# A hybrid RWKV and attention step on one core: output tiles made three at a time in the order of the input rows, and the next pair's r and v loaded in thirds

## The reference

```python
# layer 0, rwkv7_time_mix
r, k, v = rkv[0], rkv[1], rkv[2]
def step(S, inp):
    r_t, w_t, k_t, v_t, na_t, b_t = inp
    sa = jnp.einsum('bhvk,bhk->bhv', S, na_t)
    S = S * w_t[:, :, None, :] + sa[..., None] * b_t[:, :, None, :] + v_t[..., None] * k_t[:, :, None, :]
    return S, jnp.einsum('bhvk,bhk->bhv', S, r_t)
s_final, out = lax.scan(step, s0.astype(f32), xs)
...
out = (out + bonus.reshape(B, T, D)) * g
y = (out @ w_out.astype(f32)).astype(xn.dtype)
...
# layer 1, chunk_attention_prompt and chunk_attention_sample
return out @ w_out, ...
...
# every layer
hp = hp + yp
hp = hp + swiglu_ffn(rms_norm(hp, norm_ffn[layer]), ffn_w_gu[layer], ffn_w_down[layer])
```

## Time and profile before

| | us |
|---|---|
| timed runs, median of 3 | 3863.48 |
| timed runs, lowest and highest | 3858.71, 3866.56 |
| the profiled execution | 3859.63 |
| its span | 3857.9 |
| recurrence, first load to last gated store | 442.6 to 1198.8 |
| RWKV output projection, first load to first load of the next phase | 1202.9 to 1346.4 |
| attention's output projection, wide part | 2886.9 to 2953.7 |

### The profile page before, as it was taken

The page is one execution under the profiler, slowest core; times in us unless marked ns, Lnnn a source line. Parts: engine busy times, 40 slices in busy tenths (PEclk is TensorE's granted clock), DMA queues, the critical chain, the costliest instruction groups (busy, mean ns, idle before and its releaser), DMA issues. The chain is left out here.

```text
span 3857.9 us, 82894 instructions
## 1 busy us (share of the span) xinstructions
PE 3558.3 (92%) x34886; PEld 3286.7 (85%) x34886; DVE 1286.3 (33%) x2473; ACT 1002.5 (26%) x2041; POOL 1663.8 (43%) x1186
## 2 busy tenths in 40 slices
PE   7999778888885999999999999999979999999998
PEld 6999567777764999999999877777749999999997
DVE  5112456667752321122122422222232321221223
ACT  5212334445431110000000334444451100000003
POOL 5434355545532544435444543333326354444434
PEclk9999789999995999999999999999989999999999
DMA  3422101111103111111111223323331111111111
GB/s 141 136 90 83 61 22 36 46 42 36 36 23 131 40 48 44 43 38 44 43 43 38 92 69 94 98 83 90 89 119 38 50 46 41 43 38 45 42 38 55
DMA packets 289882, 234.86 MB, mean 61 GB/s; under 512 B 31619, under 2 KB 267411, under 8 KB 288838
## 3 DMA queue, kind: packets, MB, share of 16 engines
q1 hardware_dynamic: 286034, 216.55, 18.2%
q10 hardware_dynamic: 3572, 14.33, 0.9%
HBM read 188.28 MB, written 47.80 MB: 61 GB/s over the span
## 5 line engine op out<-in xcount | busy, mean ns | idle before, releaser
L1926 PE MATMUL ps<-xs,work 128*128 128x384 f32 x6048 | 1051.9, 334 | 0.0
L1926 PEld LDWEIGHTS ps<-xs,work 128*128 128x128 f32 x6048 | 1048.6, 188 | 0.0
L1891 POOL TENSOR_SCALAR work<-work 128x1024 fp32r<-128x1024 f32 x130 | 361.2, 2779 | 938.3 <-PE ps L1939 394.5
L1939 PE MATMUL ps<-work,work 128*128 128x384 f32 x2880 | 502.4, 334 | 0.0
L1939 PEld LDWEIGHTS ps<-work,work 128*128 128x128 f32 x2880 | 499.5, 188 | 0.0
L1148 PE MATMUL ps<-arena 64*64 64x64 f32 (+2 forms) x8800 | 432.6, 237 | 58.6 <-issue 15.5
L1148 PEld LDWEIGHTS ps<-arena 64*64 64x64 f32 x8800 | 324.7, 137 | 94.3 <-issue 38.9
L2417 PE MATMUL ps<-xs,work 128*128 128x384 f32 x1656 | 376.0, 358 | 2.6 <-POOL work L2355 2.6
L2044 DVE TENSOR_TENSOR H<-ps,H 128x1152 f32<-128x1152 f32 x160 | 217.2, 1358 | 479.8 <-PE ps L1939 479.8
L553 PE MATMUL ps<-mixed,wsplit_mix 128*128 128x384 f32 x1872 | 336.0, 340 | 18.3 <-DVE mixed L749 17.7
L1892 POOL TENSOR_TENSOR work<-work,work 128x1024 fp32r<-128x1024 f32 x130 | 346.1, 2662 | 10.9
(11 more groups left out here) (255 smaller groups left out, 4394.8 us busy)
## 6 DMA issues: line engine op xcount, KB each, us to landing
work<-in_ffn_w_gu SPq DMA_DIRECT2D x88, 512.0 KB, 3.8
work<-in_ffn_w_down SPq DMA_DIRECT2D x44, 512.0 KB, 3.2
work<-in_cache_v SPq DMA_DIRECT2D x64, 256.0 KB, 3.7
work<-in_cache_k SPq DMA_DIRECT2D x64, 256.0 KB, 2.8
rkv_scratch<-lora ACTq DMA_DIRECT2D x24, 576.0 KB, 2.8
arena<-rkv_scratch SPq DMA_DIRECT2D x24, 576.0 KB, 4.7
stage_mix<-in_rwkv_w_rkv SPq DMA_DIRECT2D x24, 512.0 KB, 4.0
work<-in_attn_w_qkv SPq DMA_DIRECT2D x24, 512.0 KB, 4.2
```

Source lines behind the costliest of these rows:

```text
L1891: chain.link(pool.tensor_scalar(w[:, 0, :], mem.stage3[:, slot, :], 1.0, None, ALU.mult))
L1926: last = pe.matmul(ps3[:, c, 0:CW], w[:, part, k * P:(k + 1) * P], mem.xs[:, xpart, k, c * CW:(c + 1) * CW], start=(k == 0 and a == 0), st ...
L1939: last = pe.matmul(BANKS[bank][:, c, 0:CW], mem.wsplit3[:, slots[b], part, k * P:(k + 1) * P], mem.hid[:, b, xpart, c * CW:(c + 1) * CW], ...
```

## The change

**Order of the output projection.** `OutProjection.tensor` now goes over k outside for the first three tiles: behind row k come tile 0 and tile 1 of that row, and tile 2 of row k - 2 (`LAG = 2`). Each unit is six matmuls. Tile 2 has banks 2 and 5, which the narrow parts use later, and is added to H by two operations, one for each bank. Tiles 3 to 7 follow one by one as before, with banks 0, 1 and 3, 4 by turns. Both projections use this class.

**Data in `project_phase`.** Weight tile 0 is split by ACT and DVE ahead of the rows, no longer by POOL, which begins with tile 1. Loads 1 and 2 stand ahead of rows 1 and 3. H comes in two parts, blocks 0 to 2 and then 3 to 7, with load 3 between them.

**Recurrence.** r and v come in three loads of 384 columns each. For all pairs but the first, each of the six waits until the one before it has landed; the readers wait for all six.

```diff
 class OutProjection:
+    BANKS = [(0, 1), (3, 4), (2, 5), (0, 1), (3, 4), (0, 1), (3, 4), (0, 1)]
+    LAG = 2
...
     def tensor(self, pe, tile_ready, x_ready):
         mem, norm = self.mem, self.norm
+
+        def wide(m, k):
+            for a, (w, part) in enumerate(PASSES):
+                for c in range(2):
+                    last = pe.matmul(mem.ps[:, self.BANKS[m][c], 0:CW], self.tiles[m][w][:, k * P:(k + 1) * P],
+                                     mem.xs[:, part, k, c * CW:(c + 1) * CW], start=(k == 0 and a == 0), stop=(k == KB - 1 and a == 2))
+            if k == KB - 1:
+                last.then_inc(self.done, 1)
+
+
+        for k in range(KB + self.LAG):
+            if k < KB:
+                x_ready(k)
+                for m in range(2):
+                    if k == 0:
+                        tile_ready(m)
+                    wide(m, k)
+            if k == self.LAG:
+                tile_ready(2)
+            if k >= self.LAG:
+                wide(2, k - self.LAG)
+        for m in range(3, KB):
+            tile_ready(m)
+            pe.wait_ge(self.left, m - 2 if m < 5 else m - 1)
+            for k in range(KB):
+                wide(m, k)
         for m in range(KB):
-            tile_ready(m)
-            if m >= 2:
-                pe.wait_ge(self.left, m - 1)
-            for k in range(KB):
-                if m == 0:
-                    x_ready(k)
...
-            last.then_inc(self.done, 1)
-        for m in range(KB):
-            if m >= 2:
-                pe.wait_ge(self.left, KB + m - 1)
+            pe.wait_ge(self.left, KB + m - 1 if m >= 2 else 3)
...
             dve.wait_ge(self.done, m + 1)
-            dve.tensor_tensor(h, mem.ps[:, 3 * (m % 2):3 * (m % 2) + 2, 0:CW], h, ALU.add).then_inc(self.left, 1)
+            first, second = self.BANKS[m]
+            if second == first + 1:
+                dve.tensor_tensor(h, mem.ps[:, first:second + 1, 0:CW], h, ALU.add).then_inc(self.left, 1)
+            else:
+                dve.tensor_tensor(h[:, 0, :], mem.ps[:, first, 0:CW], h[:, 0, :], ALU.add)
+                dve.tensor_tensor(h[:, 1, :], mem.ps[:, second, 0:CW], h[:, 1, :], ALU.add).then_inc(self.left, 1)
...
                 cols = slice(q * P, (q + 1) * P)
-                for j, dst in ((0, m.r), (2, m.v)):
-                    sp.dma_start(dst, mem.rkv_dram[j, cols, :]).then_inc(rv_in, 16)
+                for n, (j, dst) in enumerate(((0, m.r), (2, m.v))):
+                    for c in range(3):
+                        if q and n + c:
+                            sp.wait_ge(rv_in, 16 * (6 * q + 3 * n + c))
+                        sp.dma_start(third(dst, c), third(mem.rkv_dram[j, cols, :], c)).then_inc(rv_in, 16)
...
             def load(n):
-                if n >= 2:
-                    sp.wait_ge(w_split, n - 1)
+                if n == 2:
+                    sp.wait_ge(w0_split, 1)
+                elif n > 2:
+                    sp.wait_ge(w_split, n - 2)
...
-                if k == 1:
+                if k == 0:
                     load(1)
-            sp.dma_start(mem.H[:, :, :], mem.h_dram.rearrange("p (k n) -> p k n", k=KB)).then_inc(h_in, 16)
-            for n in range(2, KB + 2):
+                elif k == 2:
+                    load(2)
+            h = mem.h_dram.rearrange("p (k n) -> p k n", k=KB)
+            sp.dma_start(mem.H[:, 0:3, :], h[:, 0:3, :]).then_inc(h_first, 16)
+            load(3)
+            sp.dma_start(mem.H[:, 3:KB, :], h[:, 3:KB, :]).then_inc(h_rest, 16)
+            for n in range(4, KB + 2):
                 load(n)
...
         def _(act):
+            act.wait_ge(w_load[0], 16)
+            act.copy(targets[0][0], mem.stage[:, 0, :]).then_inc(w0_high, 1)
...
         def _(dve):
+            dve.wait_ge(w0_high, 1)
+            dve.tensor_tensor(targets[0][1], mem.stage[:, 0, :], targets[0][0].bitcast(F32), ALU.subtract).then_inc(w0_split, 1)
```

More of the change, by code:

```diff
@@ L252, in tensor @@
         mem, norm = self.mem, self.norm
-        for m in range(KB):
-            tile_ready(m)
-            if m >= 2:
-                pe.wait_ge(self.left, m - 1)
-            for k in range(KB):
-                if m == 0:
-                    x_ready(k)
-                for a, (w, part) in enumerate(PASSES):
-                    for c in range(2):
-                        last = pe.matmul(mem.ps[:, 3 * (m % 2) + c, 0:CW], self.tiles[m][w][:, k * P:(k + 1) * P],
-                                         mem.xs[:, part, k, c * CW:(c + 1) * CW], start=(k == 0 and a == 0), stop=(k == KB - 1 and a == 2))
-            last.then_inc(self.done, 1)
-        for m in range(KB):
-            if m >= 2:
-                pe.wait_ge(self.left, KB + m - 1)
+        def wide(m, k):
[21 more added lines that the diff above has]
+                wide(m, k)
+        for m in range(KB):
+            pe.wait_ge(self.left, KB + m - 1 if m >= 2 else 3)
             for k in range(KB):
@@ L1085, in _ @@
                     pool.wait_ge(decays_ready, 3 * pr + 1)
-                    pool.wait_ge(rv_in, 32 * pr + 32)
+                    pool.wait_ge(rv_in, 96 * pr + 96)
                     if pr >= 2:
@@ L1498, in _ @@
                     dve.wait_ge(kkn_ready, pr + 1)
-                    dve.wait_ge(rv_in, 32 * pr + 32)
+                    dve.wait_ge(rv_in, 96 * pr + 96)
                     if pr >= 2:
@@ L1598, in project_phase @@
         sem = phase_semaphores(nc, ctx, "project")
-        row_in, h_in, hi_done, lo_done = [sem("row_in0"), sem("row_in1")], sem("h_in"), sem("hi_done"), sem("lo_done")
+        row_in, hi_done, lo_done = [sem("row_in0"), sem("row_in1")], sem("hi_done"), sem("lo_done")
+        h_first, h_rest, w0_high, w0_split = sem("h_first"), sem("h_rest"), sem("w0_high"), sem("w0_split")
         w_load, w_split, pool_chain = [sem("w_load0"), sem("w_load1")], sem("w_split"), sem("pool_chain")
@@ L1629, in _ @@
             for n, (high, low) in enumerate(targets):
+                if n == 0:
+                    continue
                 pool.wait_ge(w_load[n % 2], 16 * (n // 2) + 16)
@@ L1638, in _ @@
         def _(pe):
-            proj.tensor(pe, lambda m: pe.wait_ge(w_split, m + 1), lambda k: pe.wait_ge(lo_done, k + 1))
+            proj.tensor(pe, lambda m: pe.wait_ge(w_split, m) if m else pe.wait_ge(w0_split, 1), lambda k: pe.wait_ge(lo_done, k + 1))
         @block.scalar
         def _(act):
+            act.wait_ge(w_load[0], 16)
+            act.copy(targets[0][0], mem.stage[:, 0, :]).then_inc(w0_high, 1)
             for k in range(KB):
@@ L1652, in _ @@
                 dve.tensor_tensor(mem.xs[:, 1, k, :], mem.grow[:, k % 2, :], mem.xs[:, 0, k, :].bitcast(F32), ALU.subtract).then_inc(lo_done, 1)
-            proj.vector(dve, lambda m: dve.wait_ge(h_in, 16))
+            proj.vector(dve, lambda m: dve.wait_ge(h_first if m < 3 else h_rest, 16))
 class TailNorm:
```

## The result

The changed kernel took **3834.12 us** (median of 4 runs, 3833.32 to 3840.06) beside 3865.02 us (4 runs, 3858.71 to 3868.95) for the kernel before in the same comparison: a ratio of 0.993, interval 0.991 to 0.9951, or 30.9 us less. The profiled execution took 3834.27 us with a span of 3831.9 us, 25.4 us less than the profiled execution of before (3859.63). The forecast was 3837 us in 3826 to 3850, worked out as 24.6 us less than that execution.

A forecast was written before the change was run, and what follows sets the result against it. TensorE, busy 92% of the span, was taken as the bound, so only its waits and low clock could shrink: -16.0 + 1.4 - 10.0 = -24.6 us from 3859.63 gives 3835.0, plus half of 3.85: 3837 us, range 3826 to 3850.

The forecast's parts named there:

- The two terms: Forecast gains of 16.0 us in the RWKV output projection and 10 us in the recurrence.
- RWKV projection: RWKV output projection: third tile made while rows arrive, clock rises, weights come earlier; gain 16.0 us, bounds none to 21.
- The rival of the low clock: RWKV output projection: clock stays low between rows or weights come late; gain 4 instead of 16, 3849 us; chance 0.12.
- Attention: Attention's output projection: TensorE waits for POOL's split of tile 2's weights, wanted earlier; cost 1.4 us, bounds 0 and 3.
- The bound of 3 us: Attention's output projection: upper bound of the cost, twice the wait, should the clock fall.
- Recurrence: Recurrence: loading r and v in thirds removes TensorE's stalls and the clock lost with them; gain 10 us, bounds 3 and 14.
- No issue wait above 1.3 us: Recurrence: expected sign of success, TensorE waits that the profile does not explain all staying at or below 1.3 us.
- The reading "instruction stream": Recurrence: TensorE's unexplained waits of 2.75 to 3.21 us are its next instruction block held up behind r and v data.
- The slower rival: Recurrence: thirds stretch the collision, 25 fetches at 2 us each; 25 us more, 3886 us; chance 0.04.
- SyncE's own waits are hidden: Recurrence: six thirds at 5 us each take 30 us, ending before the next keys' issue with 10 us over.

The follow-up runs named there:

- experiment 7: Changed kernel with r/v in sixths, attention projection's old order, tile 1 one row behind tile 0, weight load 4 before H's second part: 3835.47 us.

## Why the prediction was right

**The total** came out 25.4 us lower in profiled executions for a forecast of 24.6, and the median of 3834.12 lies 2.9 below 3837. The two terms that make it up were off in opposite directions, by 4.0 and 3.7 us; that the sum came out within 1 us is luck. The medians of the timed runs, with their own scatter, differ by 30.9.

**RWKV projection: right in mechanism, 2 to 4 us short in size.** In the times of before (5.97 us more, by the stage's first load) three tiles were done at 1244.3, forecast 1244.5, and the clock rose at 1223 for a forecast of 1225. The last row was split at 1234.1 instead of 1237.9: TensorE started 2.3 us earlier than before, the rows kept their 3.3 us, and the two loads ahead of rows 1 and 3, for which I had put the last row back by 1.5 us, cost them nothing. Two errors cancelled there, since a wait that I had not seen came in: 3.70 us for tile 1's weights, which POOL had in hand only at 1205.04 and whose subtraction then ran for 3.21 us instead of 2.34. Behind the three tiles I had tile 3 wait 1 to 3 us; its weights had landed at 1231.6 (1237.6 in before's times, forecast 1241), and no wait came. The wide parts ended at 1286.2 in before's times, forecast 1288.7. That is 18.5 instead of 16.0. Another 1.5 us came in the narrow part, which I had not looked at: behind its 2.1 us wait 24 matmuls ran in 4.44 us, in before in 5.99, so there too the clock stayed up. This part is chance: of the six other kernels with the new order and the new data in this stage, four have a narrow part as long as before's (40.2 us) and two a longer one (41.7 and 41.8). The pair of traces shows the change at its best. The stage takes 128.3 to 130.2 us in the six (the further one of experiment 7 left out), the three others with the stage as in before 145.5 to 147.7; by the means with the pair itself the gain is 18. The rival of the low clock is refuted for three tiles a row, and shown for one by the kernel with new data and old order.

**Attention: +1.5 for +1.4.** The wait came where it was put, and 1.18 us long. That it came at all is luck: it vanishes when the stage starts at half clock, as in nine of the fourteen traces, and both executions compared here happened to start at full clock. The bound of 3 us, for a falling clock, is not borne out by any trace.

**Recurrence: the term mis-sized.** I took the stalls to vanish with what follows them, 10 us. They shrank to what a block boundary costs in a dense stretch: after, boundaries 4.8 to 5.2 us apart wait 0.7 to 1.7 us, and the pair of before at 1106.61 and 1111.18 does so with the DMA engines at 2%. "No issue wait above 1.3 us" was wrong twice (1.36 and 1.71), and the store distances are 81.0 to 84.7, not 81 to 82. I had taken 81.31 us, the shortest distance, for what every pair takes without a stall; without any of these loads the six take 80.4 to 84.3. So the two pairs with the longest stalls gained 3.8 and 2.5 us (85.59 to 81.78 and 85.83 to 83.32) instead of 4.3 and about 4, the one with the third 0.6 (83.65 to 83.09) instead of 2.3, and the one right behind the first two lost 1.4. The gain is 6.3 us in this pair of traces and 5 in the mean of all; the timed runs of the thirds alone say 16 (8 to 24), and 10 lies between. The recurrence without any of these loads, 743.0 us, makes 13.2 the most that could be won, and the thirds took 6 of it. The reading "instruction stream" was right and is now shown by the half-block shift; that the full engines hold it up is neither shown nor refuted.

**The slower rival** (each fetch behind a third costs 1 us or more) did not come, but not by much at the places where TensorE waits: the loads stretched over 14 us, and nine boundaries, two or three in each of four pairs, wait 0.7 to 1.7 us, a mean of 1.05. The other pairs' boundaries do not wait so long, where the rival had counted 25 in all. Without the loads only 3.8 us of such waits are left, for 12.2 with the thirds. That SyncE's own waits are hidden was right, by 21 us.

## What to carry to other kernels

When input trickles in, put enough work behind each piece that TensorE has no gap before the next (here one tile's six matmuls a row left gaps and ran at 0.50, three tiles' eighteen had none and ran at 1.00). But such an order needs its other operands early: the order without the earlier weights lost 7.0 us, the weights without the order gained 9.2, both together 20.0. When an engine waits for nothing that the profile names, count its instructions between such waits: even distances mean blocks of the instruction stream, and large loads issued just before are worth cutting (here 576 KB into 192 or less), whether or not they then go one at a time. Stage lengths of traces tell apart what totals of a few runs cannot, but one trace a kernel is little when a stage itself scatters by 9 us, and a forecast confirmed by one pair of traces should be looked for in the others.

## What was not expected

- Issue waits of 0.7 us and more fall only at boundaries of 256 instructions of TensorE: 123.1 matmuls of the recurrence, and shifted by half a block by 128 more instructions.
- Two boundaries 4.57 us apart cost 1.24 us at the second, with the DMA engines at 2%.
- Behind loads of 576 KB three boundaries of the recurrence cost 2.1 to 3.2 us each; behind the same bytes as three queued loads mostly 1 (one of 2.25).
- 128 TensorE instructions that only wait, all but the first on a raised semaphore, put the recurrence off by 13 us, 0.1 us each.
- Timed runs of the unchanged kernel on one core spread from 3843.50 to 3868.61 us, and the mean granted clock goes with them (0.972 to 0.963). No trace here shows what sets it.
- The same stage begins at a granted clock of 1.00 in some executions and of 0.50 in others, whatever the order of its matmuls, and is 1.3 to 1.6 us longer in the second case where nothing else waits.
